# Turning the value product of attention round: probabilities stationary, values moving

## The reference: one encoder layer

```
def one_block(qblk):
    s = jnp.einsum('bqhgd,bkhd->bhgqk', qblk, k).astype(jnp.float32) * scale
    p = jax.nn.softmax(s, axis=-1)
    return jnp.einsum('bhgqk,bkhd->bqhgd', p.astype(v.dtype), v)
```

## Time and profile before

| | |
|---|---|
| median of 3 runs | 3203.1 us (3201.27 to 3205.05) |
| the profiled execution, its own time | 3203.52 us |
| its span, first to last instruction | 3201.7 us |
| TensorE busy over the span | 3086.6 us (96%) |
| VectorE, ScalarE, GpSimd busy | 1804.2, 1446.9, 417.4 us (56%, 45%, 13%) |
| mean granted TensorE clock | 0.983 of full speed |
| stage B's steps | about 282 to 700 us of the span |

### The profile page before, as it was taken

The page is one execution under the profiler, slowest core; times in us unless marked ns, Lnnn a source line. Parts: engine busy times, 40 slices in busy tenths (PEclk is TensorE's granted clock), DMA queues, the critical chain, the costliest instruction groups (busy, mean ns, idle before and its releaser), DMA issues.

```text
span 3201.7 us, 43742 instructions
## 1 busy us (share of the span) xinstructions
PE 3086.6 (96%) x15912; PEld 2612.5 (82%) x15912; DVE 1804.2 (56%) x1880; ACT 1446.9 (45%) x1807; POOL 417.4 (13%) x373
## 2 busy tenths in 40 slices
PE   7998999999976999999999999999999999999996
PEld 6997998978865888888888888888888888888885
DVE  6545887875665554545445455554545545455468
ACT  3225887871123444444444444444444444444464
POOL 2544241311122000000000000000000000001000
PEclk9998999999988999999999999999999999999998
DMA  6331010112245566565656656566565656656575
GB/s 210 124 107 52 11 31 25 40 54 112 114 147 173 181 213 189 205 210 183 211 185 212 213 187 210 181 212 202 191 211 182 214 188 211 211 182 212 183 262 211
DMA packets 371531, 532.71 MB, mean 166 GB/s; under 512 B 36720, under 2 KB 311920, under 8 KB 371440
## 3 DMA queue, kind: packets, MB, share of 16 engines
q1 hardware_dynamic: 356560, 488.50, 45.1%
q0 software_dynamic: 10656, 38.80, 4.7%
q10 hardware_dynamic: 4224, 4.19, 0.4%
HBM read 470.62 MB, written 60.82 MB: 166 GB/s over the span
## 4 chain that ended last, share of the span: by engine, by line
PE 86%; issue 5%; DVE 3%; POOLq 2%; POOL 1%; ACT 1%; DMA 1%; DVEq 1%; ACTq 0%; SPq 0%
PE ps_gu L902 43%; PE ps_y L940 20%; PE ps_o L790 6%; PE ps_pv L726 4%; PE ps_t L715 4%; PE ps_s L680 2%; PE ps_s L681 2%; PE ps_x L916 2%; PE ps_m L735 1%; PE ps_x L879 1%; POOLq L1664 1%; POOLq L1672 1%; PE ps_l L807 1%; POOL qkv L1678 1%; PE ps_m L666 0%
## 5 line engine op out<-in xcount | busy, mean ns | idle before, releaser
L1521 DVE TENSOR_TENSOR w_l<-w_raw,w_h 128x2048 fp32r<-128x2048 f32 x380 | 871.1, 2292 | 783.7 <-ACT w_h L1180 783.7
L1180 ACT ACTIVATE w_h<-w_raw 128x2048 fp32r<-128x2048 f32 x384 | 734.4, 1912 | 583.4 <-PE ps_gu L902 369.3
L902 PE MATMUL ps_gu<-w_h,x_h 128*128 128x512 f32 x2048 | 809.5, 395 | 0.0
L902 PE MATMUL ps_gu<-w_h,x_l 128*128 128x512 f32 x2048 | 799.7, 390 | 0.0
L902 PE MATMUL ps_gu<-w_l,x_h 128*128 128x512 f32 x2048 | 798.9, 390 | 0.0
L902 PEld LDWEIGHTS ps_gu<-w_h,x_l 128*128 128x128 f32 x2048 | 384.8, 188 | 81.3
L902 PEld LDWEIGHTS ps_gu<-w_l,x_h 128*128 128x128 f32 x2048 | 385.5, 188 | 76.2
L902 PEld LDWEIGHTS ps_gu<-w_h,x_h 128*128 128x128 f32 x2048 | 385.1, 188 | 76.4 <-DVE hf L1602 0.2
L940 PE MATMUL ps_y<-w_h,hh 128*128 128x512 f32 x1024 | 323.2, 397 | 0.0
L940 PE MATMUL ps_y<-w_l,hh 128*128 128x512 f32 x1024 | 316.7, 391 | 0.0
L940 PE MATMUL ps_y<-w_h,hl 128*128 128x512 f32 x1024 | 316.3, 390 | 0.0
(11 more groups left out here) (254 smaller groups left out, 3997.4 us busy)
## 6 DMA issues: line engine op xcount, KB each, us to landing
w_raw<-in_w_gate SPq DMA_DIRECT2D x256, 512.0 KB, 3.6
w_raw<-in_w_up SPq DMA_DIRECT2D x256, 512.0 KB, 4.7
w_raw<-in_w_down SPq DMA_DIRECT2D x128, 1024.0 KB, 4.9
xin<-in_x SPq DMA_DIRECT2D x16, 512.0 KB, 5.7
xln_d<-xln SPq DMA_DIRECT2D x16, 512.0 KB, 5.2
res<-xln_d SPq DMA_DIRECT2D x16, 512.0 KB, 3.2
h_d<-hid SPq DMA_DIRECT2D x16, 512.0 KB, 2.7
acc_d<-acc SPq DMA_DIRECT2D x16, 512.0 KB, 2.6
```

The lines of the kernel that those rows point to most:

```text
L902: last = nc.tensor.matmul(out_gu, a[:, k, tok], w[:, kk, :], start=k == 0 and q == 0, stop=k == KD - 1 and q == 2)
L1180: nc.scalar.activation(w_h[:, c % RING, :], w_raw[:, c % RING, :], ACT.Copy).then_inc(w_hi, 1)
L1521: nc.vector.tensor_tensor(w_l[:, c % RING, :], w_raw[:, c % RING, :], w_h[:, c % RING, :].bitcast(f32), ALU.subtract).then_inc(w_lo, 1)
```

## The change

The value product is turned round. The stationary operand is now a 128 by 128 tile of `pt_h` or `pt_l` (128 keys by 128 queries) and the moving operand is `v_hl` (128 columns), so that the result has queries on partitions and the two halves side by side in a row. One tile of queries is multiplied in every step, one step after it was made. ScalarE copies the two tiles of a block from `ps_pv` to `o_hl`, now at the start of an odd step; VectorE adds the halves in SBUF (`o_sum`) and multiplies by the reciprocal into `at_tok`. `add_halves`, its turn of `ps_m`, `ident2` and its two transfers go. `v_hi_copy` moves to the start of a slot's step 1, and `v_lo_sub` ahead of the step's two subtractions. VectorE waits for `o_ready`, and for `back`'s transposes before it overwrites `at_tok`; `back` waits for the new semaphore `at_ready`.

```diff
 def after_step(t, start):
-    pv = t // 2 - 1 if t % 2 == 0 else None
+    pv = t - 1
     add = (t - 3) // 2 if t % 2 == 1 else None
     back = (t - 4) // 2 if t % 2 == 0 else None
...
# TensorE
-def values(b):
-    pe.wait_ge(pt_lo, 2 * (NSTEP * s + 2 * b + 2))
-    if b == 0:
+def values(t):
+    b, c = divmod(t, 2)
+    pe.wait_ge(pt_lo, 2 * (NSTEP * s + t + 1))
+    if t == 0:
         pe.wait_ge(v_split, s + 1)
-    if not (first and b == 0):
+    if c == 0 and not (first and b == 0):
         pe.wait_ge(o_ready, NQB * s + b)
     for k in range(GT):
         for n, pt in enumerate((pt_h, pt_l)):
-            last = nc.tensor.matmul(ps_pv[:, 0:QB], v_hl[:, k, :], pt[:, b % 2, k, :],
-                                    start=k == 0 and n == 0, stop=k == GT - 1 and n == 1)
+            last = nc.tensor.matmul(ps_pv[:, c, :], pt[:, b % 2, k, c * P:(c + 1) * P],
+                                    v_hl[:, k, :], start=k == 0 and n == 0, stop=k == GT - 1 and n == 1)
     last.then_inc(pv_done, 1)
-def add_halves(b):
-    pe.wait_ge(o_ready, NQB * s + b + 1)
-    m_turn(("add", b))
-    for c in range(2):
-        last = nc.tensor.matmul(ps_m[:, c, 0:HD], o_hl[:, b % 2, c * P:(c + 1) * P], ident2[:, :],
-                                start=True, stop=True)
-    last.then_inc(m_full, 1)
 def back(b):
+    pe.wait_ge(at_ready, NQB * s + b + 1)
     m_turn(("back", b))
...
# ScalarE, at the start of a step
+    if add is not None:
+        act.wait_ge(pv_done, NSTEP * s + 2 * add + 2)
+        nc.scalar.activation(o_hl[:, add % 2, :, :], ps_pv[:, 0:2, :], ACT.Copy).then_inc(o_ready, 1)
+    if t == 1 and not first:
+        v_hi_copy(s, False)
...
-    if pv is not None:
-        act.wait_ge(pv_done, NQB * s + pv + 1)
-        nc.scalar.activation(o_hl[:, pv % 2, :], ps_pv[:, 0:QB], ACT.Copy).then_inc(o_ready, 1)
-        if pv == -1:
-            v_hi_copy(s, False)
...
# VectorE
-        lo(t)
         if t == 1 and not first:
             v_lo_sub(s)
+        lo(t)
...
+        dve.wait_ge(o_ready, NQB * s + add + 1)
         nc.vector.reciprocal(rinv[:, j:j + 2], rsum[:, j:j + 2])
+        nc.vector.tensor_tensor(o_sum[:, :, :], o_hl[:, add % 2, :, 0:HD], o_hl[:, add % 2, :, HD:P], ALU.add)
         dve.drain()
-        dve.wait_ge(m_full, turn_no(s, last_s, ("add", add)) + 1)
-        nc.vector.tensor_tensor(at_tok[:, i:i + 2, (h % 2) * HD:(h % 2 + 1) * HD], ps_m[:, 0:2, 0:HD],
+        if h % 2 == 0 and not (first and add < GT // 2):
+            gone = add - GT // 2
+            dve.wait_ge(m_full, (turn_no(s, last_s, ("back", gone)) if gone >= -2 else
+                                 turn_no(s - 1, False, ("back", gone + NQB))) + 1)
+        nc.vector.tensor_tensor(at_tok[:, i:i + 2, (h % 2) * HD:(h % 2 + 1) * HD], o_sum[:, :, :],
                                 rinv[:, j:j + 2].unsqueeze(2).to_broadcast([P, 2, HD]),
-                                ALU.mult).then_inc(m_free, 1)
+                                ALU.mult).then_inc(at_ready, 1)
```

More of the change, by code:

```diff
@@ L161, in encoder_layer @@
         pt_l = sb("pt_l", [P, 2, GT, QB], f32r)
-        o_hl = sb("o_hl", [P, 2, QB])
+        o_hl = sb("o_hl", [P, 2, 2, P])
+        o_sum = sb("o_sum", [P, 2, HD])
         at_tok = sb("at_tok", [P, GT, 2 * HD])
@@ L166, in encoder_layer @@
         rinv = sb("rinv", [P, 2 * GT])
-        ident2 = sb("ident2", [P, HD])
         upad = sb("upad", [P, SEQ + 2 * PAD])
@@ L175, in encoder_layer @@
         ps_t = [pb(f"ps_t{i}", [P, 4, P]) for i in range(2)]
-        ps_pv = pb("ps_pv", [P, 512])
+        ps_pv = pb("ps_pv", [P, 4, P])
         ps_m = pb("ps_m", [P, 4, P])
@@ L323, in encoder_layer @@
         pt_hi, pt_lo, pv_done, o_ready = sem("pt_hi"), sem("pt_lo"), sem("pv_done"), sem("o_ready")
+        at_ready = sem("at_ready")
         m_full, m_free = sem("m_full"), sem("m_free")
@@ L356, in after_step @@
                 back = None
-            return tuple(None if b is not None and (b < 0 and start or b >= NQB) else b for b in (pv, add, back))
+            if pv >= NSTEP or pv < 0 and start:
+                pv = None
+            return (pv,) + tuple(None if b is not None and (b < 0 and start or b >= NQB) else b for b in (add, back))
         def turns_of(last):
@@ L364, in turns_of @@
                 found += before_step(t, last)
-                _, add, back = after_step(t, False)
-                found += [("add", add)] if add is not None else []
+                _, _, back = after_step(t, False)
                 found += [("back", back)] if back is not None else []
@@ L372, in encoder_layer @@
         first_turns = [("Q", 0, 0), ("Q", 0, 1)]
-        TURN0 = len(first_turns) - 3
+        TURN0 = len(first_turns) - 2
         def turn_no(s, last, what):
@@ L483, in _ @@
                 sp.wait_ge(u_st[tt], 8 * PAIRS)
-            for dst, src in ((ident2[0:HD, :], eye[0:HD, 0:HD]), (ident2[HD:P, :], eye[0:HD, 0:HD]),
-                             (edge_t[:, :, :, :], pool_edge.rearrange("p (w s n) -> p w s n", w=NW, s=2)),
+            for dst, src in ((edge_t[:, :, :, :], pool_edge.rearrange("p (w s n) -> p w s n", w=NW, s=2)),
                              (wp_sb[:, :, :], w_pool.rearrange("w c d -> c w d")),
@@ L756, in stage_b @@
                         transposes(t)
-                    pv, add, bk = after_step(t, first)
+                    pv, _, bk = after_step(t, first)
                     if pv is not None:
                         values(pv)
-                    if add is not None:
-                        add_halves(add)
                     if bk is not None:
@@ L765, in _ @@
             steps(pe, SLOTS, stage_b)
+            pe.wait_ge(b_const, 48)
             for n in range(GROUPS * NW):
@@ L1036, in v_hi_copy @@
                 if not first:
-                    act.wait_ge(pv_done, NQB * s)
+                    act.wait_ge(pv_done, NSTEP * s)
                 nc.scalar.activation(v_hl[:, :, 0:HD], v_raw[:, :, :], ACT.Copy).then_inc(v_hi, 1)
@@ L1078, in hi @@
                         act.wait_ge(t_done, 2 * (NSTEP * s + t) + r + 1)
-                        if t % 2 == 0 and r == 0 and not (first and b < 2):
-                            act.wait_ge(pv_done, NQB * s + b - 1)
+                        if r == 0 and not (first and t < 4):
+                            act.wait_ge(pv_done, NSTEP * s + t - 3)
                         nc.scalar.activation(pt_h[:, b % 2, 4 * r:4 * r + 4, (t % 2) * P:(t % 2 + 1) * P],
@@ L1088, in stage_b @@
                 for t in range(NSTEP + (3 if last_s else 0)):
+                    _, add, bk = after_step(t, first)
+                    if add is not None:
[3 more added lines that the diff above has]
+                        v_hi_copy(s, False)
                     if t < NSTEP:
@@ L1120, in mix_hi @@
                 nc.scalar.activation(mx_h[:, sl, NW:KM, :], mix_pl[:, :, cols], ACT.Copy).then_inc(mx_hi, 1)
-            act.wait_ge(b_const, 80)
+            act.wait_ge(b_const, 48)
             wo_after = {0: (3,), 2: (4, 5), 4: (6, 7)}
@@ L1438, in pool_scale_up @@
                                         ALU.mult).then_inc(pl_dve, 1)
-            dve.wait_ge(b_const, 80)
+            dve.wait_ge(b_const, 48)
             pool_scale_up(1)
@@ L1738, in _ @@
             split_q(1)
-            pool.wait_ge(b_const, 80)
+            pool.wait_ge(b_const, 48)
             nc.gpsimd.memset(upad[:, 0:PAD], 0.0)
```

3 lines of the change are left out of this document (1 added, 2 removed).

## The result

The changed kernel takes 3275.6 us in the median of four runs (3275.1 to 3275.9), beside 3202.2 us for the kernel before: ratio 1.0228 [1.021, 1.0245], 73.4 us or 2.3% slower. Its profiled execution took 3275.9 us, 1.8 more than its span of 3274.1, against 3203.5 for that of before: +72.4 us. The forecast was 3283 (3222 to 3318), slower.

The account below looks back on a forecast made before the run. TensorE's instruction stream was taken to set stage B's pace. 3203.5 + 78 (more products, less `add_halves`) + 4 (slot starts) - 2 (end) = 3283.5, given as 3283 us, 2.5% slower; range 3222 to 3318.

Parts of the forecast that it names:

- What bounds the kernel: Stage B: TensorE's instruction stream sets the pace, so each microsecond added to it or taken from it counts in full.
- The price of a product: Value product in stage B: 32 products a block at 0.112 us, as the router's loads; 3.58 us a block.
- the transposes' 0.087: Rival, value product: loads are as fast as the float32r transposes', 0.087 us a product; +27 us, 3232 us; chance 0.09.
- The row that I called deciding: Value product's recorded load duration, 192 ns like the router's, against the transposes' 139; used to choose 0.112 us.
- The rival of more than one pass: Value product: each turned product runs as two pairs of load and matmul; +308 us, 3513 us; chance 0.11.
- the rival "not slower": Value product: load hides behind 128 columns, 0.066 us each, 3189 us; gains below 0.074 us a product; chance 0.05.
- `add_halves`: Removed from TensorE's stream in stage B: 0.44 us per block of two steps.
- The slot starts: First value product of a slot waits some 1.4 us for the new `v_hl`, in three slots; +4 us.
- The end: Last block of stage B: its first half is multiplied during the first wait; some 2 us back.
- VectorE and `o_hl`: Stage B: new addition of 0.292 us, 19 us in all, hidden by idle time; waiting for the `o_hl` copy costs nothing.
- the waits that I counted at nothing: TensorE's waits for `ps_m`'s turns in stage B, 2.5 us, may shrink; nothing was counted.
- The clock: Rival, stage B: granted clock falls under 1.00, losing far more than the other terms; with the rest, chance 0.03.

## Why the prediction was right, step by step

**What bounds the kernel.** Borne out: TensorE stays at 99% while the others' shares fall, and 70.8 of 72.4 us lie ahead of stage C.

**The price of a product.** Borne out, and it is the step on which all hung. From the starts of all 2048 loads to the next, without the pause at the loop's turn, the trace adds up to 230.2 us, 0.1124 each, for 229 forecast; the 1024 products before add up to 122.6 (forecast 122.9). The router's price was right against the transposes' 0.087, and the experiments with 64 and 256 columns (0.111 and 0.119) show that columns don't set it up to 128, and hardly up to 256. That it is the load which sets it, as I wrote, is not shown: every product here brings a load of its own, so the runs price the pair.

The row that I called deciding, the recorded duration of the load (192 ns against 139), was a lucky guide. A row that I left out speaks against it as a rule:

```profile
L715 PEld LDWEIGHTS ps_t<-ident,prob x1024: 137/140/232, 282.4 to 693.8; 128*128 128x128 f32 x171
```

These float32 transposes of the kernel before have loads of 140 ns, as short as those of the float32r transposes, and yet follow each other in 0.109 us in the median, not in 0.087. The prediction also does not say that its two rows of 0.112 and 0.110 are of float32 products, which are two pairs each (the router's 240 records are 15 tiles of 8 products, made twice); that a pair of the float32r value product would cost the same was carried over, and came true.

The rule of the Trainium skill (TensorE: Matmul & The Clock Gate, "Back-to-back issue gap") that would have given 81 ns a product is not borne out for this type of operand: 112 ns, and 111 even with 64 columns. The rival of more than one pass falls with one record for each product, the rival "not slower" with 0.112 against its 0.074.

**`add_halves`.** Its loads, summed the same way without the turn's pause and without the 2.7 us of waits at the stage's end that fall among them, were 28.6 us, where one block's row gave 28. So the product's terms net 230.2 - 122.6 - 28.6 = +79.0, for +78.

**The slot starts.** 3.9 us of waits, where 0.6 stood in the kernel before, so +3.3 for +4; the experiment with the low part first turns the 3.9 into 1.5.

**The end.** The waits of the last steps were 0.8, 1.3, 0.8 and 0.5 us before, 3.4 in all; after they are 0.2 and one of 1.7. So -1.5 for -2. The 1.3 and 0.8 of the earlier trace rows went as forecast; what I had not priced is that `back` of the last block now waits 1.7 us for `at_tok`, in place of 0.5, with the copy, the sum and the multiply to come one after the other behind the last product.

**VectorE and `o_hl`.** The addition takes 272 ns in the median for the 292 taken; no load waits for it in the stage, nor for `o_hl`, as forecast. Three more show that this cover gives out where GpSimd stretches them.

**The mis-sized term** is the waits that I counted at nothing. The pause at the turn lost 1.6 us and the turns of `ps_m` 2.1 ("may shrink; I count nothing"). With them the sum is 79.0 + 3.3 - 1.5 - 1.6 - 2.1 = +77.1, against 70.8 ahead of stage C. Most of the other 6.3 us is a term that I did not see: the way from the transposes to `add_halves`. In the kernel before, its first load starts 63 times behind the last transpose's, 11.5 us in sum; a value product starts 0.109 us behind it in the median, which would make 6.9. These 4.6 us went with the line (why it starts so late no run shows; made twice, its products leave this sum at 11.5). Shorter waits of the transposes for issue are another 1.6 (2.0 us in 12 from 290 to 690 before, 0.4 in 2 from 290 to 765 after). That all but 0.1 us is then placed is in part luck, since the stage's first load of scores alone starts 1.0 us later in the changed kernel (277.20 for 276.24). Behind the start of stage C, where the two kernels are the same, the changed one is 1.6 us longer; that I can't place. So the forecast, 7 to 8 us too high, had its large terms right and counted at nothing several small ones, most of which went the change's way.

**The clock.** I named a clock under 1.00 in the stage as a sign against me, and it is there: 0.83 from 530 to 540, behind the turn's pause and the wait for `v_hl` that ended at 531.02, and 0.83 from 650 to 660, behind the one that ended at 654.03. But the sign was badly chosen, for the kernel before has it too, behind its own turn:

```profile
490.00:494.00 4.00, 3.93 (x16) 3.50 (x17) 1.76 (x2) 0.98 (x2) 0.00 (x0) 0.57 0.02 6
```

As clock that was not granted it is an estimated 3.4 us after against 0.43 x 4 = 1.7 before. The rival had the right sign and was worth some 1.7 us, already inside the distances above.

## What to carry to other kernels

On a stage that TensorE bounds, count products, not columns: from 64 to 256 moving columns a product with a 128 by 128 float32r tile went from 0.111 to 0.119 us here, so an orientation that halves the columns and doubles the products pays nearly the double. To price an unseen shape, here an ordinary product was the better row even with other columns and another type (the router's 16 columns, 0.112) than a transpose with the same columns and type (0.087). And look for cover in the step where the work lands: 29 us more of VectorE's work in a stage with 80 us idle still made 63 waits, and three additions of 0.27 us that most blocks hid came through where GpSimd stretched them.

## What the hardware showed that I had not expected

**The clock behind the loop's turn and behind a wait.** At the turn TensorE pauses for 2.1 to 2.3 us in all kernels with the turned product, and the clock granted behind it differs. From 490 to 590 it was 1.00 (2.4 GHz throughout) in the one with twice the columns, 0.98 in the change, and 0.86 in the one with half the columns; in the last, nearly all of 520 to 550 was at the lower level (1.2 GHz). The kernel before, whose pause of 3.8 us is the longest, had 0.57 from 490 to 494 and 1.00 from 494 to 690, so little that its whole stretch has 1.00 in the mean. So the length of the pause alone doesn't tell what the clock does behind it. The waits of 1.3 us for `v_hl` don't either: in the change the lower level follows the one that ends at 654.03, with twice the columns the same waits stand and the clock is 1.00 from 290 to 785. These are single profiles, and the two runs of the kernel with half the columns differ by 10 us, with mean clocks of 0.977 and 0.982; what decides it is left open.

**VectorE's addition stretches beside GpSimd.** Most `o_sum` take 0.27 us, six of 64 take 0.46 to 1.56. One of them, and the GpSimd instruction that it lies beside (start, us, engine):

```profile
310.20 1.56 DVE L1412 TENSOR_TENSOR o_sum<-o_hl 128x128 f32<-128x128 f32 x1
```

```profile
309.70 1.91 POOL L1721 TENSOR_TENSOR win_a<-upad 128x1039 f32<-128x1039 f32 x1 [6.55 <-DMA upad<-ut_d]
```

The addition, with both inputs in SBUF, ends 0.15 us after GpSimd's own of two inputs, and so does each of the six, 0.14 to 0.15 us after a GpSimd instruction that had begun before it. The new multiply, now also with both inputs in SBUF, is stretched in the same way four times, to 1.36 to 1.98 us. The old multiply, which read PSUM, took 0.292 us in the mean and never more than 0.293. The Trainium skill (Advanced Engine Details and Errata, "GPSIMD Details") states that GpSimd shares a read and a write interface with VectorE, and that this conflicts with VectorE instructions that have two inputs in SBUF; the trace agrees, 0.27 against 1.56 us. Here the cover took nearly all of it: the mean of `o_sum` is 0.340 us, 64 of them 22 us for the 19 forecast, the mean of the multiply is 0.391 for 0.292, and no load of TensorE's waits for either before the stage's last block.
